# Pooled groups beside the u chunks, and half of the first gate's products between the turned probabilities

## The reference, cut to what matters

```python
z = rms_norm(x, ln1) @ w_in          # columns: u (512) | q | k | v | indexer | gates (2048)
# branch A: for group gi with window w = 2, 4, 8, 16 over u (128 channels each)
cs  = cumsum(ug); win = cs - shifted(cs, w)
d   = win / count - ug
a_pool = concat(d @ pool_w[gi]) * pool_scale
# branch B: sample rows: indexer -> top 256 keys -> gathered attention
probs = softmax(q . k_sel + bias); out = probs @ v_sel
# merge
m = sigmoid(gates[:, :1024]) * (a_pool @ w_pool_proj) + sigmoid(gates[:, 1024:]) * (a_attn @ w_attn_proj)
```

## Time and profile before

| | us |
|---|---|
| median of three runs | 1586.05 |
| the profiled execution | 1583.69 |
| its span | 1581.9 |
| busy in the span: PE / PEld | 1510.3 / 1389.8 |
| busy in the span: DVE / POOL / ACT | 935.8 / 605.5 / 561.1 |

### The profile page before, as it was taken

How to read it: one execution, slowest core, us unless ns; L and a number is a source line. 1 busy time by engine, 2 the same in 40 slices (tenths; PEclk the granted TensorE clock), 3 DMA queues, 4 the chain that set the end, 5 groups by cost and what they waited for, 6 DMA issues and landing times.

```text
span 1581.9 us, 26175 instructions
## 1 busy us (share of the span) xinstructions
PE 1510.3 (95%) x9681; PEld 1389.8 (88%) x9681; DVE 935.8 (59%) x2173; ACT 561.1 (35%) x1131; POOL 605.5 (38%) x532
## 2 busy tenths in 40 slices
PE   7998996988999999999999999999999999999997
PEld 6873896556996677999999999999999999999997
DVE  5427987689975775223539655455555454555546
ACT  4325564222215665223335422422314224132233
POOL 4112149351445221111114734626437245263350
PEclk9999998989998999999999999999999999999999
DMA  6364020234110012320102211202102011021003
GB/s 218 111 189 167 21 42 1 59 98 164 41 41 1 2 41 80 94 68 28 41 27 80 81 47 34 80 2 78 53 27 80 27 53 53 27 80 53 27 4 118
DMA packets 101494, 100.30 MB, mean 63 GB/s; under 512 B 18278, under 2 KB 91638, under 8 KB 100893
## 3 DMA queue, kind: packets, MB, share of 16 engines
q1 hardware_dynamic: 93607, 88.14, 17.5%
q0 software_dynamic: 2688, 8.39, 1.7%
q10 hardware_dynamic: 5118, 2.69, 0.6%
HBM read 86.75 MB, written 12.68 MB: 63 GB/s over the span
## 4 chain that ended last, share of the span: by engine, by line
PE 58%; DVE 1%; POOL 1%; issue 1%; ACT 0%; POOLq 0%; DVEq 0%
PE banks L2047 28%; PE banks L2144 16%; PE banks L109 13%; DVE yo L2621 0%; PE banks L2004 0%; PE banks L1985 0%; PE banks L2161 0%; POOL wL L2195 0%; ACT XH L2263 0%; POOL hnL_lo L2208 0%; DVE hnL_hi L2476 0%; POOL dL L2192 0%; POOL T4L L2208 0%; ACT sH L2256 0%; ACT resid L2260 0%
## 5 line engine op out<-in xcount | busy, mean ns | idle before, releaser
L2195 POOL TENSOR_TENSOR wL<-w_raw,wH 128x512 fp32r<-128x512 f32 x176 | 231.3, 1330 | 315.1 <-ACT wH L2306 313.9
L2047 PE MATMUL banks<-hnH,wH 128*128 128x344 f32 x704 | 225.9, 321 | 2.2 <-POOL wL L2195 0.8
L2047 PE MATMUL banks<-hnH,wL 128*128 128x344 f32 x704 | 224.8, 319 | 0.0
L2608 DVE TENSOR_TENSOR resid<-resid,banks 128x344 f32<-128x344 f32 x264 | 132.1, 512 | 96.7 <-PE banks L2144 96.7
L2144 PE MATMUL banks<-aH,dH 128*128 128x344 f32 x528 | 169.3, 321 | 0.0
L2144 PE MATMUL banks<-aH,dL 128*128 128x344 f32 x528 | 169.1, 320 | 0.0
L2144 PE MATMUL banks<-aL,dH 128*128 128x344 f32 x528 | 168.3, 319 | 0.0
L1502 DVE TENSOR_SCALAR_CACHE_REDUCE pta<-SC,thr 128x512 uint8<-128x512 f32 (+4 forms) x160 | 144.0, 930 | 2.8 <-DVE thr L1476 0.5
L2306 ACT ACTIVATE wH<-w_raw 128x512 fp32r<-128x512 f32 x176 | 109.6, 626 | 73.3 <-PE banks L2047 40.5
L2047 PEld LDWEIGHTS banks<-hnH,wH 128*128 128x128 f32 x704 | 132.1, 188 | 3.2 <-issue 1.9
L2047 PEld LDWEIGHTS banks<-hnH,wL 128*128 128x128 f32 x704 | 132.3, 188 | 0.0
(11 more groups left out here) (420 smaller groups left out, 3719.2 us busy)
## 6 DMA issues: line engine op xcount, KB each, us to landing
w_raw<-in_w_gate_up_dram SPq DMA_DIRECT2D x22, 1024.0 KB, 4.9
d_raw<-in_w_down_dram SPq DMA_DIRECT2D x11, 1024.0 KB, 4.8
big<-in_w_in_dram SPq DMA_DIRECT2D x12, 512.0 KB, 3.8
ZL<-x_lows SPq DMA_DIRECT2D x2, 2064.0 KB, 12.9
XL<-x_lows SPq DMA_DIRECT2D x2, 2064.0 KB, 7.6
W<-in_x_prompt_dram SPq DMA_DIRECT2D x8, 512.0 KB, 5.4
x_lows<-xnL SPq DMA_DIRECT2D x8, 512.0 KB, 3.6
slab_raw<-in_w_in_dram SPq DMA_DIRECT2D x8, 512.0 KB, 4.1
```

The lines of the kernel that those rows point to most:

```text
L2047: last = mm(out, W_[w][s][:, i * P:(i + 1) * P], x_of(x)(i), start=start and i == 0 and j == 0, stop=stop and i == HALF - 1 and j == 2)
L2195: gp.tensor_tensor(wL[s].rearrange("p (k n) -> p k n", k=HALF), quadrant(x, *HOME[name]), f32(wH[s]).rearrange("p (k n) -> p k n", k=HALF) ...
L2608: V.tensor_tensor(resid[:, m, chunk(DOWN_ORDER[o])], resid[:, m, chunk(DOWN_ORDER[o])], ps[:, 4 + n % 4, 0:CH], ALU.add).then_inc(y_done, 1)
```

## The change

- The four pooled groups no longer start together. PE turns the state behind chunk 4 instead of 12, ACT copies it behind u's chunk 4, and POOL makes each group when its own three u chunks are out. POOL's low halves of slabs 4 and 5 stand ahead of groups 2 and 3, those of slabs 6 and 7 behind group 3.
- To make room, slabs 2 and 3 of u use the places of the q slabs, and slabs 0 and 1 lie so that a pooled group covers only a slab that is used up. Slabs 2 and 3 are split earlier on ACT and POOL.
- Gate slab 0 has a raw place of its own (`first_gate_raw`, over `ZI` and `ZR`). SP loads it behind slab 6's low half. ACT writes its high part at projection chunk 22, POOL its low part behind DVE's last step for the probabilities.
- Gate chunks 0 to 2 are cut in half. The first 12 matmuls of each stand behind turns 1, 2 and 3; the other 12 behind `sample_values`. Gate slab 1 is loaded behind turn 3, as before; slab 2 right behind it.

```diff
-ZI = sb("ZI", [P, 576])
+ZI, ZI_at = sb_at(ctx, "ZI", [P, 576])
 ZR, ZR_at = sb_at(ctx, "ZR", [P, 512])
+assert ZR_at == ZI_at + 4 * 576
+first_gate_raw = place("first_gate_raw", 0, [D], F32, ZI_at)
...
-uH = [place(f"uH{s}", NG * UW + D * s, [D], F32R, UD_at) for s in range(2)]
-uL = [place(f"uL{s}", NG * UW + D * (2 + s), [D], F32R, UD_at) for s in range(2)]
+uH = [place(f"uH{s}", NG * UW + 2 * TOK * s, [D], F32R, UD_at) for s in range(2)]
+uL = [place(f"uL{s}", NG * UW + 2 * TOK * s + D, [D], F32R, UD_at) for s in range(2)]
...
 def uq_slab(n):
-    return {"hi": (uH if n < UQ_SLABS // 2 else qH)[n % 2], "lo": (uL if n < UQ_SLABS // 2 else qL)[n % 2]}
+    return {"hi": (uH if n < 2 else qH)[n % 2], "lo": (uL if n < 2 else qL)[n % 2]}
...
     for m in range(KD):
+        if m == 2:
+            sp.wait_ge(slab_lo, POOL_PIECES + 7)
+            sp.dma_start(first_gate_raw[:, :].rearrange("p (k n) -> p k n", k=KD), w_in_t[:, :, C_G:C_G + P]).then_inc(big_in[0], 16)
         if m >= 2:
             sp.wait_ge(p_ready, 3 * (m - 1))
         sp.dma_start(small[:, m % 2], wpp_t[:, :, m * P:(m + 1) * P]).then_inc(small_in[m % 2], 16)
...
     sp.wait_ge(sm_made, SM["probs_turned"])
-    for g in range(2):
-        load_slab(g, slice(C_G + g * P, C_G + (g + 1) * P))
+    load_slab(1, slice(C_G + P, C_G + 2 * P))
...
             transpose_sample_scores()
+        if x == 4:
+            transpose_state()
         if x == 3 * U_ITEMS:
-            transpose_state()
             transpose_last_u()
...
+    def gate_rows(x, first, end):
+        m, c = divmod(x, NCH)
+        for a in range(first, end):
+            k = G_ORDER[a]
+            for j, (w, v) in enumerate((("hi", "hi"), ("hi", "lo"), ("lo", "hi"))):
+                last = mm(ps[:, x % ROT, 0:CH], G_[w][m % 2][:, k * P:(k + 1) * P], X_[v][:, k, chunk(c)],
+                          start=(a == 0 and j == 0), stop=(a == KD - 1 and j == 2))
+        return last
+
     for q in range(1, 4):
         turn_probs(q)
+        if q == 1:
+            pe.wait_ge(slab_lo, LO_BEFORE_GATES + 1)
+            pe.wait_ge(x_lo_in[0], 32)
+        pe.wait_ge(p_evac, PROJ - 4 + q)
+        gate_rows(q - 1, 0, KD // 2)
     turn_new_prob()
     sample_values()
-
-
-    for m in range(KD):
-        s = m % 2
-        pe.wait_ge(slab_lo, LO_BEFORE_GATES + m + 1)
-        for c in range(NCH):
...
-            last.then_inc(g_ready, 1)
+    pe.wait_ge(x_lo_in[1], 32)
+    for x in range(NCH):
+        gate_rows(x, KD // 2, KD).then_inc(g_ready, 1)
+    for x in range(NCH, NCH * KD):
+        if x % NCH == 0:
+            pe.wait_ge(slab_lo, LO_BEFORE_GATES + x // NCH + 1)
+        if x < ROT:
+            pe.wait_ge(p_evac, PROJ)
+        else:
+            pe.wait_ge(g_evac, x - ROT + 1)
+        gate_rows(x, 0, KD).then_inc(g_ready, 1)
...
         pool.wait_ge(slab_hi, PIECES + n + 1)
-        if n % 4 >= 2:
+        if n >= 4:
...
     low_uq(2)
+    low_uq(3)
...
-    for n in (3, 4, 5):
-        low_uq(n)
-    pool.wait_ge(uq_evac, 3 * U_ITEMS)
+    pool.wait_ge(nat_ready, NT)
+    gp.memset(U[:, :, 0:16], 0.0).then_inc(pool_fill, 1)
+    pool.wait_ge(sidx_used, NB)
     pool.wait_ge(stT_evac, 1)
-    pool.wait_ge(sidx_used, NB)
-    gp.memset(U[:, :, 0:16], 0.0).then_inc(pool_fill, 1)
-    did(gp.tensor_copy(sx[:, :, :, POOLBUF], U[:, :, 16 + SEQ:16 + TOK]))
     pool.wait_ge(pool_fill, 3)
     for g in range(NG):
+        if g >= 2:
+            low_uq(g + 2)
+        pool.wait_ge(uq_evac, 3 * (g + 1))
+        did(gp.tensor_copy(sx[:, g, :, POOLBUF], U[:, g, 16 + SEQ:16 + TOK]))
...
         pool.wait_ge(pooled, g + 1)
-        if g < 2:
-            low_uq(6 + g)
+    low_uq(6)
+    low_uq(7)
     pool.wait_ge(sm_step, STEP["list"])
     for c in range(16):
...
     def low_slab(m):
         pool.wait_ge(slab_hi, HI_BEFORE_GATES + m + 1)
-        gp.tensor_tensor(gL[m % 2][:, :], raw[:, m % 2, :], f32(gH[m % 2][:, :]), ALU.subtract).then_inc(slab_lo, 1)
+        if m == 0:
+            pool.wait_ge(sm_step, STEP["new_prob"])
+        gp.tensor_tensor(gL[m % 2][:, :], raw[:, m % 2, :] if m else first_gate_raw[:, :], f32(gH[m % 2][:, :]), ALU.subtract).then_inc(slab_lo, 1)
...
-        if n % 4 >= 2:
+        if n >= 4:
...
+    high_uq(2)
...
     act.wait_ge(causal_done, NSEL)
+    high_uq(3)
...
-    HIGH_AT = {2: 2, 5: 3, 7: 4, 10: 5, 14: 6, 17: 7}
+    HIGH_AT = {8: 4, 11: 5, 14: 6, 17: 7}
...
         u_out(x)
+        if x == 4:
+            act.wait_ge(stu_turned, 1)
+            A(sx[:, :, :, 0:POOLBUF], ps[:, 6, 0:480].rearrange("p (g b t) -> p g b t", g=NG, b=NB), ACT.Copy).then_inc(stT_evac, 1)
...
-    act.wait_ge(stu_turned, 1)
-    A(sx[:, :, :, 0:POOLBUF], ps[:, 6, 0:480].rearrange("p (g b t) -> p g b t", g=NG, b=NB), ACT.Copy).then_inc(stT_evac, 1)
...
-        A(gH[m % 2][:, :], raw[:, m % 2, :], ACT.Copy).then_inc(slab_hi, 1)
+        A(gH[m % 2][:, :], raw[:, m % 2, :] if m else first_gate_raw[:, :], ACT.Copy).then_inc(slab_hi, 1)
...
             sample_exp()
+        if x == 22:
+            act.wait_ge(pool_out, 48)
+            high_slab(0)
         if x == 23:
             probs_out(0)
...
         probs_out(q)
     new_prob_out()
-    high_slab(0)
     values_out()
     high_slab(1)
```

More of the change, by code:

```diff
@@ L813, in _ @@
                 for q in range(1, 4):
                     turn_probs(q)
+                    if q == 1:
[3 more added lines that the diff above has]
+                    gate_rows(q - 1, 0, KD // 2)
                 turn_new_prob()
                 sample_values()
-                for m in range(KD):
-                    s = m % 2
-                    pe.wait_ge(slab_lo, LO_BEFORE_GATES + m + 1)
-                    for c in range(NCH):
[L823 to L831, removed]
-                                last = mm(ps[:, x % ROT, 0:CH], G_[w][s][:, k * P:(k + 1) * P], X_[v][:, k, chunk(c)],
-                                          start=(a == 0 and j == 0), stop=(a == KD - 1 and j == 2))
-                        last.then_inc(g_ready, 1)
```

## The result

The changed kernel takes 1575.36 us, the median of six runs (1573.17 to 1578.40); the kernel before took 1587.12 in six runs beside them (1583.82 to 1593.06). The ratio is 0.9916, 95% interval 0.9894 to 0.9939, which is 13.3 us less (9.7 to 16.8; the two medians alone are 11.8 apart). In a second set of runs (e12) it is 0.9928 [0.9902, 0.9954]. Forecast were 1578.5 and a range of 1572.5 to 1584.5.

The account below looks back on a forecast made before the run. PE was taken to bound the kernel (58% of the chain). -3.3 and -4.4 give -7.7 us: 1583.69 becomes 1576.0, plus 2.4 to the median 1578.4, stated as 1578.5; range 1572.5 to 1584.5.

Parts of the forecast that it names:

- part 1: Pooled groups made behind their own u chunks: the wait for the last group goes, slabs come later; -3.3 us.
- part 2: Gate chunks 0 to 2 cut in half: two waits and a fall of the clock go; -4.4 us.
- POOL's sum: POOL's work from 194.5 to slab 6's low half at 250.1, so PE starts chunk 18 9.4 us later.
- The fall of the clock behind it: PE's slow clock behind its wait for a low half at chunk 18, put at 1.6 us.
- DVE's chain: Running sum behind the ties, 7.7 us before, loses 3.2 with POOL idle; new PE wait 0.1 us.
- The halves: Gate halves between turns and behind values: waits of 1.1 and 1.7 and slow clock of 1.6 go; slabs fit by about 1 us.
- The stretch of slow issue: 7.8 us in the projection in which PE waits for nothing visible; could move a few us, left to the range.
- The rival of -18.8: The q slabs come in time and PE starves for nothing: -14.4 - 4.4, 1567 us; chance 0.05.
- The slower rival: POOL's work stretched beside DVE, slab 6 18 us later: +10.3, 1596 us; chance 0.08.

Follow-up runs that it names:

- e12: The changed kernel again, with no edit: 1575.46 us, ratio 0.9928 to the kernel before.
- e6: Changed kernel with slab 5's low half inside group 2 and those of slabs 6 and 7 inside group 3: 1563.51 us, ratio 0.9838.
- e7: e6 with ROUNDS_AHEAD 0 instead of 5: 1550.88 us, ratio 0.9752 to the kernel before.
- e10: Changed kernel with three POOL subtractions of 1024 columns added from the end of the sums of ties on: 1582.00 us, ratio 0.9958.
- e9: Kernel before with 12 extra matmuls, results unread, behind each of turns 1 to 3: 1584.48 us, ratio 0.9984.
- e11: Kernel before with 76 unread matmuls on the gate's operands in PE's wait ahead of turn 0: 1584.26 us, ratio 0.9979.
- e1: Kernel before with only the pooled-group edits, gates as before: ratio 0.9965, -5.6 us.
- e4: The kernel before again, with no edit: 1590.13 us.
- e8: Kernel before with 76 unread matmuls on plain fp32 operands in PE's wait ahead of turn 0: 1612.86 us, ratio 1.0152.

## Why the prediction was right, and where it was not

Over all traces, each stretch for the kernels with and without the part (us, mean and number):

| stretch | without | with | difference | predicted |
|---|---|---|---|---|
| first u chunk to projection (part 1) | 118.1 (6) | 115.2 (5) | -2.9 | -3.3 |
| turn 0 to attention (part 2), with the 13 us wait | 115.1 (2) | 106.4 (5) | -8.8 | -4.4 |

Kernels in which the stretch itself was altered are left out (e6, e7, e10 in the first row, e9 and e11 in the second). The second row's two without the part are e1 (111.8) and e4 (118.4); the first trace of before, with its short wait ahead of turn 0, has 110.9. Between the two stretches, from the projection to turn 0, the traces have 77.6 to 77.7 us where five rounds stand ahead of turn 0, but for the first, which has 81.4, and e8, whose filler makes it 108.3. With the first trace of before counted in, the second row's "without" is 113.7 and its difference -7.3.

- **POOL's sum**: right in every term. POOL's start and the end of slab 6's low half came as worked out, and PE's wait there is 5.37 and 6.8 us in the two traces of the changed kernel. 6 to 8 was said; the 5.37 falls short because in that trace the clock was also low behind the wait of 2.1 at chunk 15 (0.50 from 234 to 237 us), so PE came later to chunk 18. In e12 it was not.
- **The fall of the clock behind it**: mis-sized. It was put at 1.6 us, the value of the gate chunk; at chunk 18 it cost 6.64 - 3.78 = 2.9. So the mapping started only 0.5 us earlier than before by the count from the first u chunk, not 1 to 3, and part 1 gave 2.0 in this trace, not 3.3. In e12 the mapping is 0.9 earlier. The ties start 12.3 and 11.8 us later (10 to 12 was said).
- **DVE's chain**: right. The running sum ends 3.3 us behind the start of the ties (277.30 to 280.59) and not 7.7, for the reason given. The chain is 4.4 us shorter and not 3.2, since L1577 (0.86, now 0.43) and L1583 (1.07, now 0.29) had been held too, which the prediction left out; e10 brings the long instructions back, and with them a wait of 4.4 us.
- **The halves**: both slabs were in time. The term was 1.1 + 1.7 + 1.6. What these name is gone, and the trace gives 5.0. But the sum took the first trace's values, at the full clock, as the kernel's usual ones. Of six traces with neither halves nor a filler between the turns, two (e4, e8) had them at the low level for 17 to 20 us, and all six have some low clock between turn 1 and gate chunk 1; in all seven with the halves there is none (in e10 the low clock of turn 0 reaches 0.5 us into turn 1). By the times more than half of the executions of the kernel before are of the upper group. By these sizes this mis-sized term is why part 2 measures -9.5 and the whole -13.3 instead of -7.7: against the lower group alone the whole is -8.1. The sum was right for the kind of execution that it was read from. The gain was 5.6 us larger than forecast and the time 3.1 lower; that it lies in the range is owed to the range's 6 us to each side, not to a price for this term.
- **The stretch of slow issue** was left to the range as "a few us either way". It was an event of one execution, worth 3.7 us in that trace and, seen in one trace of 14, little in the medians. The forecast took the profiled execution's own 2.4 us below the median as its offset; that execution had the stretch but not the slow values.
- **The rival of -18.8** was judged by whether POOL could be faster. e6 shows that it was a matter of order: the same POOL work, 12 us more gained. In the changed kernel itself PE starved for the slabs, as forecast.
- **The slower rival**, POOL stretched by DVE, did not happen: POOL's additions took 1.92 and its low halves 2.40 beside the search rounds.

## What to carry to other kernels

When a stream of helper work feeds a bound engine at fixed points, work out the order of the stream and not only its sum: three pieces moved forward inside the same POOL list were worth as much as the whole change. A wait that vanishes in front of one step shows up at the next thing that step depends on, so look for what stands needlessly ahead of it (here five search rounds, 12 us). And take a second trace before a price that comes through the clock or through a stretch without a visible cause enters a sum. Before that, look at the times and mean clocks of all executions: two groups among them say that one trace shows only one of two cases.

## What the runs showed of the hardware

- The same wait of 2.7 us at the same product was followed by the granted clock of 0.50 for some 6 us in one execution (a loss of 2.6) and by 1.00 in another. Chunk 18's wait of 5.4 cost 2.9 more, gate chunk 0's of 1.65 cost 1.6.
- Sparse work on PE, the turns and the values, met the low level even directly behind 44 us of dense work (e8). The kernel before has two groups of times, 1580.3 to 1587.2 and 1589.7 to 1596.0 us, with mean granted clocks of 0.981 to 0.984 and 0.974 to 0.979.
- POOL's subtraction holds back a DVE instruction with two SBUF inputs until it ends (0.3 us become 2.1 to 2.4) and isn't itself slowed (2.40). One with a single tensor input can be held as well: L1481, 1.73 for 0.17. POOL's scaling of one input (2.74) let two such DVE instructions pass at 0.42 and 0.29.
- A product of plain fp32 operands, 128x344, takes 0.58 us in two records of 0.29; one of fp32r operands 0.157.
